# Two transformer blocks on one core: chunk u2 ahead of k1, evened channel norm, norm weights first and x in quarters

## The reference

```python
h = rms_norm(x, attn_norm_w)
q, k, v, u, g = split(h @ w_in)                  # 1024, 1024, 1024, 2048, 2048 columns
q = rms_norm(q, q_norm_w); k = rms_norm(k, k_norm_w)   # per group of 64
a = diff_attention(q1, q2, k1, k2, v, lam, rel_bias)   # 8 heads, two softmaxes each, causal
y_a = (rms_norm(a, subln_w) * (1 - lam_init)) @ w_proj_attn
u_a, u_b = split(u)
c = causal_depthwise_conv(u_a * sigmoid(u_b), conv_w, conv_b)   # 31 taps
y_b = silu(layer_norm(c, conv_ln_w, conv_ln_b)) @ w_proj_conv
g_a, g_b = split(sigmoid(g + gate_b))
x = x + (g_a * y_a + g_b * y_b) @ w_out
```

## Time and profile before

| | |
|---|---|
| median of 3 runs | 757.6 us (756.88 to 757.79) |
| the profiled execution | 757.69 us |
| its span, first to last instruction | 756.0 us |
| PE busy | 732.0 us, 97% |
| DVE, ACT, POOL busy | 483.0, 397.1, 176.2 us |
| granted TensorE clock | 1.00 |
| chain that ended last | PE 66%, DVE 12%, ACT 9%, POOL 6% |

### The profile page before, as it was taken

How to read it: one execution, slowest core, us unless ns; L and a number is a source line. 1 busy time by engine, 2 the same in 40 slices (tenths; PEclk the granted TensorE clock), 3 DMA queues, 4 the chain that set the end, 5 groups by cost and what they waited for, 6 DMA issues and landing times.

```text
span 756.0 us, 9087 instructions
## 1 busy us (share of the span) xinstructions
PE 732.0 (97%) x3430; PEld 596.5 (79%) x3430; DVE 483.0 (64%) x664; ACT 397.1 (53%) x521; POOL 176.2 (23%) x124
## 2 busy tenths in 40 slices
PE   6989999999999999999999999999999999999998
PEld 5767777777877888888888888877778888888886
DVE  4697885999977656555556364677746655653541
ACT  5644667565486455444445354569846445543330
POOL 1279899896700003000000000150001000000000
PEclk9999999999999999999999999999999999999999
DMA  9865545354537555655664655634334555565640
GB/s 293 228 193 194 160 132 188 118 196 153 180 113 270 177 166 173 195 189 171 198 202 142 221 176 186 223 126 153 112 112 145 186 171 174 172 211 172 219 139 29
DMA packets 81899, 131.44 MB, mean 174 GB/s; under 512 B 3888, under 2 KB 34632, under 8 KB 81856
## 3 DMA queue, kind: packets, MB, share of 16 engines
...
...
## 4 chain that ended last, share of the span: by engine, by line
PE 66%; DVE 12%; ACT 9%; POOL 6%; issue 4%; DMA 3%; SPq 0%; ACTq 0%; DVEq 0%; POOLq 0%
PE acc L1539 20%; PE acc L1541 20%; PE acc L1540 20%; DVE aux L913 5%; PE aux L1220 3%; ACT w_hi L560 3%; DMA raw<-w_in_dram 3%; POOL w_lo L545 2%; DVE w_lo L869 2%; POOL qk_r L450 2%; POOL qk_ss L462 1%; DVE gates L1050 1%; ACT conv L811 1%; DVE tok L924 0%; ACT junk L598 0%
## 5 line engine op out<-in xcount | busy, mean ns | idle before, releaser
L869 DVE TENSOR_TENSOR w_lo<-raw,w_hi 128x2048 fp32r<-128x2048 f32 x98 | 222.9, 2275 | 127.1 <-ACT w_hi L560 127.1
L560 ACT ACTIVATE w_hi<-raw 128x2048 fp32r<-128x2048 f32 (+1 forms) x119 | 225.7, 1900 | 141.3 <-PE acc L1541 130.7
L1539 PE MATMUL acc<-w_hi,h_hi 128*128 128x512 f32 x640 | 257.6, 402 | 5.3 <-DVE tok L924 3.2
L1541 PE MATMUL acc<-w_hi,h_lo 128*128 128x512 f32 x640 | 250.7, 392 | 0.0
L1540 PE MATMUL acc<-w_lo,h_hi 128*128 128x512 f32 x640 | 250.1, 391 | 0.0
L1539 PEld LDWEIGHTS acc<-w_hi,h_hi 128*128 128x128 f32 x640 | 121.1, 189 | 31.0 <-DVE tok L924 4.0
L1541 PEld LDWEIGHTS acc<-w_hi,h_lo 128*128 128x128 f32 x640 | 120.6, 188 | 26.3
L1540 PEld LDWEIGHTS acc<-w_lo,h_hi 128*128 128x128 f32 x640 | 120.9, 189 | 23.1
L545 POOL TENSOR_TENSOR w_lo<-raw,w_hi 128x2048 fp32r<-128x2048 f32 x21 | 97.7, 4656 | 2.0 <-ACT w_hi L560 2.0
L913 DVE SCALAR_TENSOR_TENSOR aux<-glu_t,vec_t,aux 128x256 f32<-128x256 f32 x232 | 94.3, 482 | 0.0
L450 POOL TENSOR_TENSOR rstd<-ms,nhalf 128x2 f32<-128x2 f32 x4 | 8.7, 2183 | 349.5 <-DVE ms L896 349.5
...
## 6 DMA issues: line engine op xcount, KB each, us to landing
...
raw<-w_gate_up_dram SPq DMA_DIRECT2D x44, 512.0 KB, 4.8
...
raw<-w_in_dram SPq DMA_DIRECT2D x16, 512.0 KB, 6.3
...
```

The lines of the kernel that those rows point to most:

```text
L560: nc.scalar.activation(w_hi[:, u % SPLIT, 0:nk, :], raw[:, u % RAW, 0:nk, :], ACT.Copy)\
L869: nc.vector.tensor_tensor(w_lo[:, u % SPLIT, 0:nk, :], raw[:, u % RAW, 0:nk, :], f(w_hi[:, u % SPLIT, 0:nk, :]), ALU.subtract).then_inc(w_ ...
L1539: nc.tensor.matmul(o, x_h, w_hi[:, slot, j, :], start=begin_, stop=False)
L1541: mm = nc.tensor.matmul(o, x_l, w_hi[:, slot, j, :], start=False, stop=end_)
```

## The change

Seven things change, all in the first 34 units:

1. Chunk order: u2 comes ahead of k1 (units 12, 13 are u2; 14, 15 are k1). Attention is started at steps 8 to 15 and 18 to 25 instead of 8 to 23, the taps per step are 11 up to step 14, 10 up to 20, then 12 (before 11 up to 8, 8 up to 16, then 13).
2. Start: the four norm weights alone (`norm_rows`, 16 KB) are loaded first and turned; x comes in quarters of columns, each followed by two k-tile pieces of units 0 and 1, and PE turns a quarter of x between k-tiles of unit 0. `vecs` and `onehot` are loaded behind unit 2 and used in the middle of unit 1.
3. The reads of `bias` stand at steps 3 to 6 (before 1 to 4).
4. For q0, k0, q1, k1 four taps stand ahead of the normalising multiplication.
5. w_lo of unit 4 stands at the head of step 2; the squares of x are made in two parts.
6. The attention output is scaled in three groups (8, 4, 4 pieces) and turned at steps 26, 27, 29.
7. Channel norm: the sums over the groups of channels are finished on DVE, so that PE makes one product for the mean and one for the variance (before three and four); the root stands at step 28, the scaling is cut in two, and the first two gate sigmoids move to step 26.

```diff
-    out = [u(0), q(0), k(0), u(1), v(0), q(1), k(1), u(2), v(1), u(3)]
+    out = [u(0), q(0), k(0), u(1), v(0), q(1), u(2), k(1), v(1), u(3)]
-    ATT = [*range(8, 24)]
+    ATT = [*range(8, 16), *range(18, 26)]
-        n = 11 if s < 9 else 8 if s < 17 else 13
+        n = 11 if s < 15 else 10 if s < 21 else 12
-        a_steps = {24: (0,), 25: (1,), 28: (2, 3)}
+        a_steps = {26: (0, 1), 27: (2,), 29: (3,)}
+        A_GROUPS = [(19, 0, 8), (26, 8, 12), (28, 12, 16)]
...
-            for t in range(NT):
-                sp.dma_start(x_in[:, t, :], x_rows[:, t, :]).then_inc(x_loaded[t], 16)
+            for g in range(UK):
+                cols = slice(256 * g, 256 * (g + 1))
+                sp.dma_start(x_in[:, :, cols], x_rows[:, :, cols]).then_inc(x_loaded[g], 16)
+                piece(g // 2, 2 * (g % 2))
+                piece(g // 2, 2 * (g % 2) + 1)
...
+                if u == PIECED:
+                    sp.dma_start(vecs[:, :], a["vectors"]).then_inc(vecs_loaded, 16)
+                    sp.dma_start(onehot[:, :], a["bucket_onehot"]).then_inc(onehot_loaded, 16)
...
-            act.dma_start(vecs[:, :], a["vectors"]).then_inc(vecs_loaded, 16)
+            act.dma_start(norm_rows[:, :], a["vectors"][R_NORM[0]:R_NORM[0] + 4, :]).then_inc(gains_loaded, 16)
...
-                for r in range(2 * s - 2, 2 * s) if 1 <= s <= step // 2 else ():
+                for r in range(2 * s - 6, 2 * s - 4) if 3 <= s <= step // 2 + 2 else ():
...
+                ahead = 0
                 for kind, i in QK:
                     if i < 2 and s == end[kind, i] + 1:
+                        ahead = min(4, quota[s] - early)
+                        for _ in range(ahead):
+                            conv_step(taps_done)
+                            taps_done += 1
                         norm_qk(kind, i)
...
+                if s == conv_last:
+                    dve.wait_ge(conv_added, 5)
+                    for n in range(2):
+                        dve.wait_ge(conv_done, CONV_OPS - 1 + n)
+                        nc.vector.tensor_tensor(conv_sum[:, :], conv_sum[:, :], conv[:, 6 + n, :], ALU.add)\
...
+                    dve.wait_ge(ln_sq, 2)
+                    for n, k in enumerate((4, 2, 1)):
+                        nc.vector.tensor_tensor(centered_sq[:, 0:k, :], centered_sq[:, 0:k, :], centered_sq[:, k:2 * k, :],
+                                                ALU.add).then_inc(sq_added, 1)
...
-                kts = (0, 6, 7) if n == 0 else range(4)
-                for kt in kts:
-                    moving = conv_sum[:, :] if n == 0 and kt == 0 else src[:, kt, :]
-                    mm = nc.tensor.matmul(aux[:, 2, 0:S], mean_w[:, :], moving, start=(kt == 0), stop=(kt == kts[-1]))
+                nc.tensor.matmul(aux[:, 2, 0:S], mean_w[:, :], src, start=True, stop=True).then_inc(ln_sum, 1)
...
-            for t in range(NT):
-                pe.wait_ge(x_loaded[t], 16)
-            stage(0, range(4))
+            stage(0, (0,))
...
+                    if s == 0:
+                        stage(0, (j + 1,) if j < UK - 1 else ())
```

More of the change, by code:

```diff
@@ L561, in split_high, with first_high, row_squares @@
                     .then_inc(w_hi_ready, 1)
-            def first_high(kt):
-                act.wait_ge(raw_in[0], raw_value[0])
-                nc.scalar.activation(w_hi[:, 0, kt, :], raw[:, 0, kt, :], ACT.Copy)\
+            def first_high(u, kt):
+                act.wait_ge(piece_in[UK * u + kt], 16)
+                nc.scalar.activation(w_hi[:, u, kt, :], raw[:, u, kt, :], ACT.Copy)\
                     .then_inc(first_hi if kt < UK - 1 else w_hi_ready, 1)
+            def row_squares(t):
+                for hf in range(2):
+                    act.wait_ge(x_loaded[2 * hf], 16)
+                    act.wait_ge(x_loaded[2 * hf + 1], 16)
+                    if t or hf:
+                        act.wait_ge(squares, 2 * t + hf)
+                    nc.scalar.activation(junk[:, :], x_in[:, t, CW * hf:CW * (hf + 1)], ACT.Square,
+                                         accum_out=ss[:, 0, hf, t:t + 1]).then_inc(squares, 1)
             def stage_high(st, g):
@@ L690, in _ @@
                             .then_inc(probs_kept, 1)
-                if (s < EARLY or s >= B) and s != LN + 3 and s not in NORMS and s + LEAD < NU:
+                if (0 < s < EARLY or s >= B) and s not in NORMS and s + LEAD < NU:
                     split_high(s + LEAD)
+                if s == 1:
+                    row_squares(1)
                 if s in ended:
@@ L949, in pv2_low, with ln_scale, a_low @@
                     .then_inc(o2_lo, 1)
-            dve.wait_ge(vec_ready, 1)
-            for kt in range(UK):
-                if kt % 2 == 0:
-                    stage_low(0, kt // 2)
-                first_low(kt)
-            stage_low(0, 2)
-            stage_low(0, 3)
-            split_low(1)
-            mean_square(0)
+            def ln_scale(hf):
+                ch = conv[:, 4 * hf:4 * hf + 4, :]
+                nc.vector.tensor_tensor(ch, ch, again(ln_r[:, :], 4), ALU.mult).then_inc(ln_y, 1)
+            def a_low(g):
+                dve.wait_ge(a_hi, g + 1)
+                nc.vector.scalar_tensor_tensor(
+                    out=y_lo[:, 2 * g:2 * g + 2, :], in0=aux[:, A_BANK[g], :].rearrange("p (a b) -> p a b", a=2),
+                    scalar=gains[:, 0:1], in1=f(y_hi[:, 2 * g:2 * g + 2, :]), op0=ALU.mult,
+                    op1=ALU.subtract).then_inc(a_lo, 1)
+            dve.wait_ge(norm_ready, 1)
+            first_low(0, 0)
+            stage_low(0, 0)
+            first_low(0, 1)
+            first_low(0, 2)
+            first_low(0, 3)
+            stage_low(0, 1)
+            first_low(1, 0)
+            first_low(1, 1)
+            stage_low(0, 2)
+            first_low(1, 2)
+            first_low(1, 3)
+            stage_low(0, 3)
+            split_low(2)
+            dve.wait_ge(vec_ready, 1)
             for i in range(2):
@@ L1370, in halfway @@
             def halfway(s):
+                if s == 1:
+                    pe.wait_ge(vecs_loaded, 16)
+                    claim([2], vec_ready, 1)
+                    for kt in range(KT):
+                        mm = nc.tensor.transpose(aux[:, 2, VROWS * kt:VROWS * (kt + 1)], vecs[:, P * kt:P * (kt + 1)],
+                                                 ident[0:VROWS, 0:VROWS])
+                    mm.then_inc(vec_turned, 1)
+                    pe.wait_ge(consts_loaded, 16)
+                    pe.wait_ge(onehot_loaded, 16)
+                    pe.wait_ge(zeros_ready, 5)
+                    claim([3], rel_kept, 1)
+                    nc.tensor.matmul(aux[0:H, 3, 0:RELS], rel_aug[:, :], onehot[:, :], start=True, stop=True)\
+                        .then_inc(rel_made, 1)
                 for i in range(4):
@@ L1432, in after @@
             def after(s):
[L1433 to L1440 removed]
+                if s == 2:
                     pe.wait_ge(lam_made, 2)
```

195 lines of the change are left out of this document (104 added, 91 removed).

## The result

The changed kernel takes 753.82 us (median of 5, 753.12 to 755.91) against 757.79 (756.88 to 760.62) for the kernel before on the same chip: ratio 0.994, 95% interval 0.9925 to 0.9955.

> The changed kernel itself beside the others, as their reference: 753.8 (753.1 to 755.9), 0.994 of the kernel before.

The account below looks back on a forecast made before the run. TensorE (PE) was taken as the bound, so only its idle time ahead of 231 us and its work could shrink: 1.7 + 2.2 + 2.1 = 6.0 us, giving 751.6 us; own range 749.8 to 753.4, stated range 747.8 to 755.8.

Parts of the forecast that it names:

- the step to unit 8: From the start to unit 8: unit 8 starts at 62.1 instead of 63.80, a gain of 1.7 us.
- the first rival: Start doesn't carry through: first transfer lands late, unit 8 gains 0 or loses 0.5; 753.0 to 755 us, chance 0.20.
- the wait for probs_t: Unit 28: PE waits 1.3 us because ACT makes the squares ahead of the last score's probs_t.
- The wait for tok: Ahead of unit 6, PE waits for normalised q0 until near 49.6; an end past 51 would show the prediction wrong.
- The first matmul: At the start: first weight matmul at 7.9 instead of 12.07 us, with the first 16 KB landing at 4.5.
- Unit 2: Unit 2 starts at about 23.4 instead of 25.95, 2.5 us earlier; the vectors are in by 17.
- Unit 6: DVE's chain for q0, with taps from 33.7, is done at 49.5; unit 6 gains 1.9 us.
- The half pace behind a wait: PE at half its matmul pace after a wait: forecast only at the start, a loss of 1.8 us kept unchanged.
- Unit 8: Unit 8 waits for k0, set by POOL: done at 60.9 counted from 45.7, normalised at 62.1.
- Channel sums and waits from unit 8 to 32: Five fewer PE products in the channel norm save 2.2 us; waits fall from 6.1 to 4.0, saving 2.1.
- DVE free: Rival: moved taps free DVE from unit 17 on, nearly all 6.1 us of waits go; 748.1 us, chance 0.20.
- overfilled: Rival: DVE overfilled in steps 9 to 14, all twenty moved taps on the path cost 7.8; 761.5 us, chance 0.10.

Follow-up runs that it names:

- after_again: The changed kernel itself, run again beside later kernels: 754.36 us, 0.9946 of the kernel before.
- filler_unit6: The changed kernel with three idle products on PE at the end of unit 5, while it waits ahead of unit 6: 754.48 us (0.9936).
- old_sums: The changed kernel with the channel norm's sums as before, three and four products on PE, without DVE's extra sums: 754.88 us (0.9942).
- new_start_alone: The kernel before with only the new start, keeping old chunk order, taps and sums: 758.37 us (0.9985).
- chain_freed: The changed kernel with vectors ahead of unit 2, q0/k0 squares earlier on ScalarE, taps put off, bias transfers issued by SyncE: 749.16 us (0.9876).

## Why the prediction was right, and where it was not

**Faster, and by the right stretch.** The forecast of 751.6 was 2.2 us too low, and the 4.3 us forecast for units 8 to 32 are 4.4. Where it failed is the step to unit 8: -1.7 forecast, +1.0 measured (+1.4 in after_again), so the whole gain of the start is missing. 753.82 lies above the forecast's own range (749.8 to 753.4) and inside that of the first rival, whose cause did not occur; that it lies in the stated range is in part luck. Of the prediction's own signs, PE's wait of 3 to 4 us ahead of unit 6, the wait for probs_t and the unchanged stretch behind unit 32 came. The wait for tok ended at 51.33, past the 51 that it had named as a sign of being wrong (50.38 in after_again), and unit 32 came 3.4 us earlier and not 6.

**The first matmul** was to come at 7.9 and came at 6.57, since the 16 KB landed by 3.09, not at 4.5; the bounds drawn from the earlier trace rows, 4.5 to 6.8, lay above. The issue stands at 0.79, so it took 2.3 us. By the Trainium skill, DMA: Bandwidth & Descriptors, section Anatomy of one DMA, a transfer issued by GpSimd has a fixed part of about 2.0 us. This one went by ScalarE's queue, for which the section gives no figure; its 2.3 us are near it, and the estimate of 2.8 was the better one. The first rival (the start doesn't carry through, 753.0 to 755) gave the time that came, but by another way than its late first transfer.

**Unit 2** at 23.4: 25.55, 23.72 in after_again, 22.98 to 27.92 over the kernels with the new start. The vectors were to be in by 17 and were in at 19.7, 11.4 us behind their issue, at 279 GB/s. But it did not decide: after_again has unit 2 1.8 earlier and unit 8 0.35 later.

**Unit 6** at 49.6: the terms for DVE were right one by one (15 taps 5.97, reduction 1.28, w_lo 2.29), but they start at 35.5, not at 33.7, so DVE is done at 51.3. This is the step that failed first: w_hi of unit 5 was to be made from 29.3, with no term for its weights. Its transfer was issued at 22.95 and took 7.9 us, until 30.9, and the lambda copy ahead of it on ACT ran only at 31.3, since it waits for the product moved behind unit 2. In after_again the transfer alone decides, at 30.4.

**The half pace behind a wait** was no term at all. I let the start keep its own and thought of none elsewhere, because unit 6 had run at full pace behind 3.03 us in the kernel before. It cost 1.5 us in unit 6 here and 2.9 in after_again (9.35 against 6.5). At unit 8 it counts for less, since tok of k0 ended at 64.2 (63.2 in after_again) and PE would have waited for it: by this estimate 0.6 of the 64.8 here, 2.0 of the 65.2 there. filler_unit6 shows the cause, and by its time nothing was gained.

**Unit 8** by POOL at 60.9 for qk_r: 62.9. The 45.7 it was counted from is 47.7, and that is the same late start: DVE's reduction of q0 ends at 42.0, where the prediction's terms give 40.2 (33.7 + 5.3 + 1.2), and the 5.5 us from there to 45.7 are what qk_ss and qk_r of q0 take (2.59 and 2.93). The two pairs of bias issues were counted rightly (2.17). So of the 2.7 us that unit 8 comes late, 2.1 are POOL's chain, which inherits DVE's delay, and 0.6 the half pace.

Ahead of unit 6 POOL was done at 47.7, PE itself at 48.2 and DVE's taps at 50.0; ahead of unit 8 tok of k0 at 64.2 and PE at 64.8. So each single repair found the next chain. By the ratios against 0.9940: vectors first 2.0 us slower, no taps ahead of tok(q0) 1.1 slower, the idle products 0.3 faster, the taps alone 1.8 faster; together 4.9 faster, and with w_lo of unit 7 off POOL 6.4. Each ratio is known to about 1 us either way: only the vectors first and the two joint repairs are clear of the changed kernel's interval (0.9925 to 0.9955).

**What the new start is worth:** on the kernel before 0.15% (0.9985), on the rest of the change 0.2% (0.9964 to 0.9940 and 0.9946, with intervals that overlap); the rest without it and without the taps ahead, 0.9930, is within the interval of the whole change. The 1.7 us forecast up to unit 8 are there at most as far as the start pays for the four taps ahead.

**Channel sums and waits from unit 8 to 32,** 2.2 and 2.1. By the books both are there: from unit 8 to 32 PE's busy time fell from 161.5 to 159.4 us and its idle time from 6.1 to 3.9. As causes they are mis-sized. old_sums, which has the five products back, loses 0.35 us up to unit 32 and not 2.2: without them PE waits for probs_t instead. new_start_alone, with the old order, taps and sums, needs 167.32 from unit 8 to 32 and the changed kernel 163.25, so of 4.1 some 3.7 come from the order, the taps and the groups, which were not run one by one. The two errors cancel: the sum was right by luck, not the split. The new sums alone on the kernel before were not run; with other waits behind them they may be worth more there. Of the single waits 0.95 in unit 14 (1.0 said), 1.76 for probs_t in unit 28 (1.3) and 0.4 at pc0 (0.4) are there; those of 0.2 in unit 18, 0.6 in unit 26 and 0.5 in unit 29 are not (each under 0.15), so POOL's price for the last group (power 1.02 us for 4 columns, products 2.91) did not reach the path; 0.3 each for probs in unit 17 and probs_t in unit 27 were not foreseen.

**DVE free (748.1)** and **overfilled (761.5)** fell: of the 6.1 us of waits 3.9 are left where the first wanted nearly none, and for the second PE idles only 1.3 us from 64 to 150, with DVE busy 70.5 of 86. chain_freed put one more tap into each of steps 8 to 14 and got no longer there.
